# One-core Trainium2 kernel of two transformer blocks: the first projection summed in two channel halves, modulation sums moved to other engines

## What is computed

```python
cond_lat = c[:, None, :]
sh1, sc1, g1, sh2, sc2, g2 = ada_terms(cond_lat, ada_w[i], ada_b[i])   # split(silu(cond) @ w + b, 6)
hl = modulate(rmsnorm(x, norm1_g[i]), sh1, sc1)                        # h * (1 + scale) + shift
yl = short_conv_mixer(hl, conv_w_in[j], conv_w[j], conv_w_out[j], True)
x = x + g1 * yl
x = x + g2 * swiglu(modulate(rmsnorm(x, norm2_g[i]), sh2, sc2), ffn_w_in[i], ffn_w_out[i])
```

## Time and profile before

| what | us |
|---|---|
| median of 3 runs (1398.75 to 1401.97) | 1398.92 |
| the profiled execution | 1401.05 |
| its span, first to last instruction | 1399.3 |
| TensorE busy / VectorE busy / ScalarE busy | 1315.8 / 831.5 / 670.7 |

### The profile page before, as it was taken

The page is one execution under the profiler, slowest core; times in us unless marked ns, Lnnn a source line. Parts: engine busy times, 40 slices in busy tenths (PEclk is TensorE's granted clock), DMA queues, the critical chain, the costliest instruction groups (busy, mean ns, idle before and its releaser), DMA issues.

```text
span 1399.3 us, 18491 instructions
## 1 busy us (share of the span) xinstructions
PE 1315.8 (94%) x6809; PEld 1101.6 (79%) x6809; DVE 831.5 (59%) x1017; ACT 670.7 (48%) x992; POOL 156.8 (11%) x121
## 2 busy tenths in 40 slices
PE   1869899999899999888999999999999999999998
PEld 1869688888788888776788888888888888788886
DVE  5998665444665555644655556655555477555554
ACT  2304343444554445544654456545544465655443
POOL 1880392000500000200000000000000100000000
PEclk9979999999999999999999999999999999999999
DMA  9967575555355556460375555555572433265551
GB/s 335 343 231 254 181 240 180 182 191 196 106 183 192 194 188 203 142 175 31 122 237 183 180 195 181 180 181 180 184 236 90 150 136 119 93 227 193 180 195 61
DMA packets 171581, 253.64 MB, mean 181 GB/s; under 512 B 9785, under 2 KB 135949, under 8 KB 171533
## 3 DMA queue, kind: packets, MB, share of 16 engines
q1 hardware_dynamic: 168352, 244.33, 52.9%
q0 software_dynamic: 2304, 8.41, 1.6%
q10 hardware_dynamic: 878, 0.25, 0.1%
HBM read 249.77 MB, written 1.05 MB: 179 GB/s over the span
## 4 chain that ended last, share of the span: by engine, by line
PE 84%; DVE 9%; ACT 3%; DMA 1%; issue 1%; POOL 0%; DVEq 0%; SPq 0%; ACTq 0%; POOLq 0%
PE ps L512 26%; PE ps L514 25%; PE ps L513 25%; DVE tmp L1575 2%; PE ps L554 2%; DVE w_lo L1372 2%; DVE x_sb L1428 1%; DMA raw<-in_ada_w 1%; PE ps L813 1%; PE ps L532 1%; DVE tmp L1423 1%; DVE tmp L1525 1%; PE ps L698 1%; ACT w_hi L1012 1%; ACT tmp L1017 0%
## 5 line engine op out<-in xcount | busy, mean ns | idle before, releaser
L512 PE MATMUL ps<-w_lo,xT_hi 128*128 128x512 f32 (+1 forms) x960 | 382.2, 398 | 4.8 <-DVE xT_lo L1453 2.7
L1372 DVE TENSOR_TENSOR w_lo<-raw,w_hi 128x2048 fp32r<-128x2048 f32 x117 | 278.1, 2379 | 166.3 <-ACT w_hi L995 166.3
L514 PE MATMUL ps<-w_hi,xT_lo 128*128 128x512 f32 (+1 forms) x960 | 374.4, 390 | 0.0
L513 PE MATMUL ps<-w_hi,xT_hi 128*128 128x512 f32 (+1 forms) x960 | 374.0, 390 | 0.0
L1377 DVE SCALAR_TENSOR_TENSOR w_lo<-raw,par,w_hi 128x512 fp32r<-128x512 f32 x336 | 230.4, 748 | 139.7 <-ACT w_hi L1000 139.5
L995 ACT ACTIVATE w_hi<-raw 128x2048 fp32r<-128x2048 f32 x117 | 223.5, 1912 | 181.8 <-PE ps L514 160.0
L512 PEld LDWEIGHTS ps<-w_lo,xT_hi 128*128 128x128 f32 x960 | 182.1, 190 | 41.9 <-DVE xT_lo L1453 3.0
L1000 ACT ACTIVATE w_hi<-raw,par 128x512 fp32r<-128x512 f32 x336 | 214.3, 712 | 0.8 <-PE ps L514 0.8
L514 PEld LDWEIGHTS ps<-w_hi,xT_lo 128*128 128x128 f32 x960 | 181.4, 189 | 38.5
L513 PEld LDWEIGHTS ps<-w_hi,xT_hi 128*128 128x128 f32 x960 | 182.2, 190 | 35.6 <-issue 0.2
L512 PE MATMUL ps<-w_lo,hT_hi 128*128 128x512 f32 x400 | 156.5, 391 | 0.0
(11 more groups left out here) (224 smaller groups left out, 1443.5 us busy)
## 6 DMA issues: line engine op xcount, KB each, us to landing
raw<-in_ffn_w_gate SPq DMA_DIRECT2D x88, 512.0 KB, 4.0
raw<-in_ffn_w_up SPq DMA_DIRECT2D x88, 512.0 KB, 4.9
raw<-in_ffn_w_down SPq DMA_DIRECT2D x88, 512.0 KB, 4.1
raw<-in_ffn_w_in SPq DMA_DIRECT2D x44, 512.0 KB, 4.7
raw<-in_conv_w_in SPq DMA_DIRECT2D x24, 512.0 KB, 5.4
raw<-in_fox_w_in SPq DMA_DIRECT2D x24, 512.0 KB, 4.3
raw<-in_ffn_w_out SPq DMA_DIRECT2D x22, 512.0 KB, 4.4
raw<-in_ada_w SPq DMA_DIRECT2D x16, 512.0 KB, 6.5
```

Of the source, the lines that this page charges most:

```text
L512: pe.matmul(o, a_hi, b_lo, start=first, stop=False, skip_group_check=True)
L513: pe.matmul(o, a_hi, b_hi, start=False, stop=False, skip_group_check=True)
L514: return pe.matmul(o, a_lo, b_hi, start=False, stop=last, skip_group_check=True)
L1372: dve.tensor_tensor(w_lo[:, slot_of(n), :], raw[:, slot_of(n), :], w_hi[:, slot_of(n), :].bitcast(F32), ALU.subtract).then_inc(raw_done, 1)
```

## The change

In the projection's first column half the input channels 0 to 511 are now taken for all three sections, then 512 to 1023; the second column half goes section by section as before. Sections 0 and 1 of the modulation are loaded in two halves (columns 0 to 511 and 512 to 1023 of each section, which are the input channels of the projection). The first half is summed on TensorE directly, with the loaded blocks as weights and a column of `cond` as the moving operand (`first_piece`). The second half and section 4 (SCALE2) are summed on TensorE in four groups of 32 columns, with a padded `cond` as weights (`column_sums`), and the groups are added with a small selection matrix `sel`. VectorE keeps section 2 (GATE1) in steps 6, 10, 11 and 15. The biases of sections 0 and 1 come in with the other parameter rows; `split` and `load` are as before, and the weight slots serve no modulation blocks any more. `CHUNK_OUT` says at which step of ScalarE's and VectorE's loop a chunk is copied out, `CHUNK_DONE` after which unit.

```diff
+        CHUNK_DONE = (3, 4, 5, 7, 9, 11)
+        CHUNK_OUT = {6: 0, 7: 1, 9: 2, 10: 3, 12: 4, 14: 5}
...
+            def load_second(i):
+                if i == 3:
+                    sp.wait_ge(xT_ps, 4)
+                dst = second_raw[i].rearrange("p k (s c) -> p k s c", s=2)
+                for j in range(2):
+                    sp.dma_start(dst[:, j, :, :], ada_1[:, 2 * i + j, :, HALF:D]).then_inc(second_landed[i], 16)
...
             def load_ada_v(q):
-                if not 0 <= q < 2 * ADA_CH:
-                    return
                 if q >= 2:
                     sp.wait_ge(ada_v_add, 2 * (q - 1))
-                c0, k = ADA_V[q // ADA_CH] * D, 2 * (q % ADA_CH)
-                sp.dma_start(ada_v_raw[:, q % 2, :, :], ada_w[:, k:k + 2, c0:c0 + D]).then_inc(ada_v_landed[q % 2], 16)
-
-            for half in range(2):
-                for section in (1, 2, 0):
-                    for k0 in (0, 4):
-                        load(n, 0, columns(n, conv_in, k0, section * D + half * 512, 512))
-                        load_ada_v(n - BASE[CONV] - 3)
-                        n += 1
+                sp.dma_start(ada_v_raw[:, q % 2, :, :], ada_w[:, 2 * q:2 * q + 2, GATE1 * D:(GATE1 + 1) * D])\
+                    .then_inc(ada_v_landed[q % 2], 16)
+
+            def load_scale2(q):
+                if q < 2:
+                    sp.wait_ge(second_ps, 1)
+                else:
+                    sp.wait_ge(scale2_ps, q - 1)
+                sp.dma_start(scale2_raw[q % 2], ada_w[:, 2 * q:2 * q + 2, SCALE2 * D:(SCALE2 + 1) * D])\
+                    .then_inc(scale2_landed[q % 2], 16)
...
+            load_first(0)
+            load_first(1)
+            sp.dma_start(x[:, :, :], x_d).then_inc(x_landed, 16)
+            load_first(2)
+            load_first(3)
+            load_first(4)
+            load_conv(0)
+            load_first(5)
+            load_first(6)
+            load_first(7)
+            load_conv(1)
+            load_conv(2)
+            load_second(0)
+            load_second(1)
+            load_second(2)
+            load_conv(3)
+            load_second(3)
+            load_conv(4)
+            load_ada_v(0)
+            load_conv(5)
+            load_scale2(0)
+            load_conv(6)
+            load_scale2(1)
+            load_conv(7)
+            load_ada_v(1)
+            load_conv(8)
+            load_scale2(2)
+            load_conv(9)
+            load_scale2(3)
+            load_conv(10)
+            load_ada_v(2)
+            load_conv(11)
+            load_ada_v(3)
+            n += 12
+            sp.wait_ge(scale2_ps, 4)
             sp.dma_start(rows[:, 0, :], w["norm2_g"].to_broadcast([P, D])).then_inc(g2_row_landed, 16)
...
+            def column_sums(pieces, k0):
+
+                for j in range(2):
+                    for h in range(2):
+                        g = 2 * j + h
+                        mm = pe.matmul(ps[32 * g:32 * g + 32, 0, :], cond32[:, k0 + j, :],
+                                       pieces[:, j, h * HALF:(h + 1) * HALF],
+                                       start=k0 == 0, stop=k0 == KT - 2, skip_group_check=True)
+                return mm
...
+            def first_piece(k):
+
+                pe.wait_ge(first_landed[k], 16)
+                for s in range(2):
+                    for c in range(4):
+                        mm = pe.matmul(ps[:, 4, 4 * s + c:4 * s + c + 1], first_raw[:, k, s, c * P:(c + 1) * P], cond[:, k:k + 1],
+                                       start=k == 0 and s == 0 and c == 0, stop=k == KT - 1, skip_group_check=True)
+                if k == KT - 1:
+                    mm.then_inc(mod_ps, 1)
...
+            pe.wait_ge(cond_ready, 1)
+            for k in range(4):
+                first_piece(k)
+            pe.wait_ge(par_landed, 224)
             pe.transpose(ps[:, 6, 0:N_PAR], par_rows[0:N_PAR, 0, :], ident[0:N_PAR, 0:N_PAR])
             pe.transpose(ps[:, 7, 0:P], par_rows[:, 1, :], ident[:, :]).then_inc(par_ps, 1)
 
             for t in range(TOKT):
+                first_piece(4 + t)
                 pe.wait_ge(xn_done, t + 1)
                 for k in range(KT):
                     tr = pe.transpose(ps[:, k // 2, (k % 2) * SEQ + t * P:(k % 2) * SEQ + (t + 1) * P], xn[:, t, tok(k)], ident[:, :])
                     if t == 1 and k % 2:
                         tr.then_inc(xT_ps, 1)
-            pe.wait_ge(raw_done, ADA_FIRST)
+            first_piece(6)
+            first_piece(7)
...
+            channel_unit(0, CONV_BANK[0], 0, ready=True)
+            pe.wait_ge(xnT_raw, 1)
+            channel_unit(1, CONV_BANK[1], 0)
+            pe.wait_ge(cond32_ok, 1)
+            pe.wait_ge(xnT_ok, 2)
+            second_piece(0)
+            second_piece(1)
+            channel_unit(2, CONV_BANK[2], 0)
+            second_piece(2)
+            second_piece(3)
+            pe.wait_ge(second_sb, 1)
+            for c in range(4):
+                mm = pe.matmul(ps[:, 1, 2 * c:2 * c + 2], second_sum[:, c * P:(c + 1) * P], sel[:, :], start=True, stop=True)
+            mm.then_inc(mod_ps, 1)
+            channel_unit(3, CONV_BANK[0], 1, ready=True)
+            channel_unit(4, CONV_BANK[1], 1)
+            channel_unit(5, CONV_BANK[2], 1)
+            pe.wait_ge(evac_a, 1)
+            channel_unit(6, CONV_BANK[3], 0)
+            scale2_piece(0)
+            channel_unit(7, CONV_BANK[3], 1)
+            scale2_piece(1)
+            pe.wait_ge(evac_v, 1)
+            channel_unit(8, CONV_BANK[4], 0)
+            scale2_piece(2)
+            channel_unit(9, CONV_BANK[4], 1)
+            scale2_piece(3)
+            pe.wait_ge(evac_v, 2)
+            channel_unit(10, CONV_BANK[5], 0)
+            pe.wait_ge(scale2_sb, 1)
             for h in range(2):
...
+                mm = pe.matmul(ps[:, h, :], sel[:, h:h + 1].to_broadcast([P, P]), scale2_sum[:, :], start=True, stop=True)
+            mm.then_inc(ada_ps, 1)
+            channel_unit(11, CONV_BANK[5], 1)
...
+                if i == 1:
+                    pe.wait_ge(ada_row_v, 1)
+                    pe.wait_ge(ada_v_add, 2 * ADA_CH)
+                    row_everywhere(0, tmp[:, 0, :])
...
             act.wait_ge(x_landed, 16)
             for t in range(TOKT):
                 root_x(0, t)
-            split(BASE[CONV])
-            for k in range(0, KT, 2):
-                act.wait_ge(xnT_ok, k // 2 + 1)
-                act.activation(xT_hi[:, k:k + 2, :], xnT[:, k:k + 2, :], ACT.Copy).then_inc(xT_hi_ok, 1)
-                if k == 0:
-                    split(BASE[CONV] + 1)
-
+            act.wait_ge(xT_ps, 4)
+            act.activation(xnT[:, 4:8, :].rearrange("p k c -> p (k c)"), ps[:, 2:4, :].rearrange("p b n -> p (b n)"),
+                           ACT.Copy).then_inc(xnT_raw, 1)
             n = BASE[CONV]
-            for k in range(2, 18):
-                m = (k - 4) // 2
-                if k % 2 == 0 and 0 <= m < 6:
-                    act.wait_ge(w_used, weight_count(n + 2 * m + 1))
+
+            def turned_pair(b):
+                act.wait_ge(xnT_ok, b + 1)
+                act.activation(xT_hi[:, 2 * b:2 * b + 2, :], xnT[:, 2 * b:2 * b + 2, :], ACT.Copy).then_inc(xT_hi_ok, 1)
+
+            split(n)
+            turned_pair(0)
+            turned_pair(1)
+            split(n + 1)
+            split(n + 2)
+            split(n + 3)
+            act.wait_ge(second_ps, 1)
+            act.activation(second_sum, ps[:, 0, :], ACT.Copy).then_inc(second_sb, 1)
+            turned_pair(2)
+            turned_pair(3)
+            for k in range(4, 18):
+                m = CHUNK_OUT.get(k)
...
+            split(n)
+            modulation(0)
+            modulated(0)
+            modulated(1)
+            turned_pair(0)
+            turned_pair(1)
+            split(n + 1)
+            split(n + 2)
+            split(n + 3)
+            modulation(1)
+            modulated(2)
+            modulated(3)
+            turned_pair(2)
+            turned_pair(3)
...
+                if k == 12:
+                    dve.wait_ge(scale2_bias, 32)
+                    dve.wait_ge(scale2_ps, 4)
+                    dve.tensor_tensor(scale2_sum, ps[:, 0, :], scale2_sum, ALU.add).then_inc(scale2_sb, 1)
+                if k in (7, 12):
+                    dve.wait_ge(evac_v, 1 if k == 7 else 3)
+                    taps(0 if k == 7 else 1, ((0, 1), (1, 0)))
+                if k == 13:
+                    dve.wait_ge(ada_ps, 1)
+                    dve.wait_ge(g2_row_landed, 16)
+                    dve.scalar_tensor_tensor(rows[:, 0, :], ps[:, 0:2, :].rearrange("p b n -> p (b n)"), 1.0, rows[:, 0, :],
+                                             ALU.add, ALU.mult).then_inc(ada_row_v, 1)
+                if k in (8, 13):
+                    taps(0 if k == 8 else 1, ((2, 2),))
+                if k in (6, 10, 11, 15):
+                    ada_chunk((6, 10, 11, 15).index(k))
...
+            pool.wait_ge(mod_ps, 1)
             ada_p_section(0)
-
```

(70 more changed lines are left out.)

156 lines of the change are left out of this document (53 added, 103 removed).

## The result

The changed kernel took 1417.26 us (median of 5 runs, 1410.49 to 1418.33) against 1399.49 (1398.75 to 1402.0) for the kernel before on the same chip: a ratio of 1.0108, 95% interval 1.009 to 1.0127. It is slower by some 15 us by the ratio, 18 by the medians; the five times spread over 8 us. The profiled execution took 1418.16 us, with a span of 1416.4.

A forecast was written before the change was run, and what follows sets the result against it. VectorE, slowed by GpSimd's sums beside it, was taken to bound the stage, TensorE waiting for `w_lo`. Shifts of +8.1 to the first output product and +3.1 in the output units gave about +11: 1410 us, range 1400 to 1415.

The forecast's parts named there:

- Front: Before the first projection product: 128 narrow instructions at 0.218 us take 27.9 us; first product at 41.0 instead of 41.89.
- Column sums: TensorE's sums of second halves and SCALE2: 0.95 us a piece, bounds 0.87 and 3.4; unit 3 starts at 68.4.
- price without a drain: Lower bound for a column-sum piece on TensorE: 8 instructions, 0.87 us, nothing added for changes of tiling mode.
- The chain: Loads, ScalarE and VectorE steps before unit 11: `scale2_sum` done at 134.2, TensorE idle 13.7 us from 120.5.
- Clock and `conv_y`: Behind that wait: slow-clock rows 3.4 and unit 11 6.2, open `conv_y` 1.22; first output product at 145.1, shift +8.1.
- Output units: After the first output product: gate row (1.7) moves in behind unit 13 and waits 1.4 more for its last chunk; +3.1.
- Everything later is untouched: Behind this stage nothing changes, so the change is worth what it shifts the end of the stage.
- unit 12's load is not late: Rival, chance 0.12: gate's fourth load goes out by 107, first output product at 129.4, kernel faster at 1394.
- Column groups in sequence: Rival, chance 0.04: TensorE's column groups run one after the other, 8 pieces x 2.5 = 20 more; 1425.
- front short: Rival, chance 0.10: narrow products raise the clock, 0.136 us each, front about 10 us shorter; 1400, no change.
- chain at its short end: Rival, chance 0.08: VectorE undisturbed by GpSimd (-3.3) and both weight landings 1 us quicker (-2); 1405.

The follow-up runs named there:

- silent_pool: Changed kernel with GpSimd's first four chunks clearing one column instead of multiplying and adding, loads and signals kept: 1411.32 us, ratio 1.0086.
- split_13_late: sum_step_10 with VectorE's split of unit 13 moved from before the last taps and `conv_y` to behind `yT_lo`: 1395.93 us, ratio 0.9972.
- late_row: Changed kernel with the SCALE2 row's broadcast and its wait moved behind unit 11 on TensorE: 1414.69 us, ratio 1.0101.
- loads_first: Changed kernel with unit 12's weights issued ahead of the gate's fourth load on SP's queue: 1409.97 us, ratio 1.0067.
- order_only: Changed kernel with unit 12's weights ahead of the gate's fourth load, `scale2_sum` at step 10, gate sums at steps 5, 9, 11, 14: 1408.67 us, ratio 1.0066.
- sum_early: Changed kernel with VectorE making `scale2_sum` at step 10 instead of step 12: 1413.53 us, ratio 1.0094.
- warm_front: Changed kernel with 14 dense products on TensorE ahead of the first narrow product: 1416.93 us, ratio 1.0119.
- packed_front: Changed kernel with the first half's modulation also summed in four column groups, over pairs of channel blocks, instead of narrow products: 1405.66 us, ratio 1.0043.
- sum_step_10: packed_front plus order_only's orders, on the changed kernel, but the third gate sum at step 10 instead of 11: 1397.54 us, ratio 0.9985.

## Why the prediction was right, and where it was short

The direction and the mechanism were right; the size was short: +11 forecast, +15 by the ratio. The median of 1417.26 lies 2 us above the range (1400 to 1415); on the 1398.92 from which the prediction started the ratio gives 1414, just inside. Of the profiled execution (1412 forecast, 1418.16) the steps say:

- **Front** (37.8, first product 41.0): narrow products end at 36.9, first product at 40.01. Right, at 0.213 us where I took 0.218.
- **Column sums** (0.95 a piece): 0.99 (91.91 to 92.90). Unit 3 at 67.30 for 68.4. The price was near, a little low: a unit and a piece take 6.94 from start to start (91.91 to 98.85), and 48 products at 0.12 leave 1.18 for the piece. Beside the price without a drain (0.87) that is some 0.15 for each of its two changes of tiling, at which starts lie 0.21 to 0.23 apart instead of 0.12. The rule of the Trainium skill (TensorEngine Tiling (Array Packing), Key Properties) that a change of mode drains TensorE would by the prediction's estimate be 0.28 for each. The trace shows about half of that, so neither the rule so priced nor "none", as the prediction read the earlier trace rows, fits.
- **The chain** (`scale2_sum` done at 134.2): 137.3, the step that was mis-sized. Two landings were too short. Unit 10's weights: "7.7 from the first issue" and a little, 110; they were issued earlier (100.39) and came at 112.1, 11.7 after it. I had priced them as 2 MB in a row with a part of GpSimd's load among them. In silent_pool, where that load went out earlier, they took 9.3: so GpSimd's 1 MB cost them 2.4, about all of its 2.5 and not the 1.0 that I had put in (101.3 to 110 is 8.7), and the row of 7.7 was too short besides. Unit 12's: 9.0 forecast, 9.8 measured (122.68 to 132.50). With the split of 3.18 for 2.85 that makes the 3.1 in the main. Besides, unit 10's weights were late enough to hold TensorE 3.62 at 117.41, which the prediction had denied ("TensorE never waits for `w_lo` now but for the chain"); it cost nothing, for the longer wait behind it took it in.
- **Clock and `conv_y`** (145.1): 148.74. Rows and unit 11 took 10.1 for 9.6; the rest is the late sum.
- **Output units** (+3.1): (174.02 - 158.84) - (148.74 - 136.99) = 3.4, of it a wait of 1.56 at the gate row (1.4 forecast).
- **"Everything later is untouched"**: 15.2 at the residual became 17.1 at the end. By VectorE's residual steps the distance is 15.2 at 367, 14.2 at 564, and 16.9 at 676 (times of before). In the attention and long convolution between them the same work ran at a lower granted clock: the kernel before, and then the changed one, in the stretch that answers.

```profile
610.00:630.00 20.00, 16.80 (x203) 11.64 (x206) 14.30 (x30) 10.13 (x26) 0.00 (x0) 0.91 0.35 120
...
650.00:676.15 26.15, 23.60 (x101) 18.79 (x99) 10.21 (x12) 13.10 (x20) 0.00 (x0) 0.87 0.26 81
```

```profile
624.20:644.20 20.00, 16.80 (x189) 11.12 (x188) 13.24 (x29) 9.06 (x24) 0.00 (x0) 0.83 0.40 141
...
664.20:693.00 28.80, 25.50 (x104) 20.51 (x104) 10.94 (x14) 13.47 (x21) 0.00 (x0) 0.82 0.23 74
```

  The same happened the other way round in split_13_late: 5.6 ahead at the residual (153.23), 3.8 at the end of the span (1395.5). Some 2 us either way hang on where the clock falls, and no experiment here steered that: from the residual to the end of the span the fourteen traces need 1238.1 (late_row) to 1242.4 us (the changed kernel), the kernel before 1240.5. So about 2 of the 17.1 us are not the change's doing in this stage, or not shown to be.

Of the rivals, *unit 12's load is not late* was tried in loads_first and order_only: without the queue's delay the output product comes at 144.5 and 141.2, not 129.4, since unit 10's weights are late by themselves, which was the reason against it, and VectorE's steps stand behind them. *Column groups in sequence* is out (0.99), *front short* too. Of *chain at its short end* silent_pool shows the size: of its 5.0 us the arithmetic on VectorE is 3.75 (2.86 in the two sums, 0.89 in the split), where 3.3 was forecast, and the rest is the earlier landing of unit 10's weights (110.77 for 112.14).

What stays open is why unit 10's weights need 9.3 us even without GpSimd's load: SCALE2's, the gate's and unit 11's loads are issued around them, and none of these was taken away.

## What to carry to other kernels

Where engines run written orders, a sum taken off the bound engine pays only if what replaces it is cheap and the loads and orders are written anew. Here narrow products cost 9.2 us at the front, and a weight load queued behind a buffer wait with a sum two steps after its use cost 7.3 at the residual; the 21 us of freed time on VectorE did not make up for that. With both mended the kernel was level with the one before, and two more changes of order made it 0.3% faster. Sum a weight matrix over its rows by column groups with the matrix as the moving operand, not as 128x128 weights for one column: 16 products instead of 64 for the same data. And when a wait goes and the time stays (late_row, sum_early), look for the next wait on the same producer.

## What the runs showed of the hardware

- One-column float32 products are not timed by their columns: 0.213 us an instruction at the slow clock, as far apart as the projection's products of 256 columns (40.58 and 40.79 in the changed kernel), and about 0.11 at the fast clock, where those are 0.12. A clock of 1.00 fell to 0.50 under them with TensorE never idle (warm_front).
- The granted clock reads 1.00 until its first fall in a trace: the changed kernel's first stretch shows 1.00, and its narrow products run at the spacing (0.213) that warm_front shows at 0.50; at 43.1 the spacing of the products goes from 0.21 to 0.12 and the record stays at 1.00. At the start of a trace the spacing tells, not the record.
- Four column groups of 512 columns: 8 instructions take 1.07 us with their tail at the fast clock (91.91), and 1.94 ahead of the projection, at what by its length is the slow one (packed_front, 6.58, where the record reads 1.00). Beside products of the other tiling they take 1.18 from start to start.
- GpSimd's sums beside VectorE cost unevenly: two gate sums 2.86 to 5.47 us instead of 2.60, a split up to 4.51 instead of 2.29 (sum_step_10).
- With a 1 MB load of GpSimd's in flight a weight unit took 11.7 us from its issue in the changed kernel (10.1 to 12.5 in five other traces), without it 9.3 (silent_pool).
